# Query weights in three equal blocks, and squares added on VectorE ahead of one sum on TensorE

## What is computed

```python
def _rms(x, g):
    y = xf * lax.rsqrt(jnp.mean(xf * xf, axis=-1, keepdims=True) + EPS)
    return y * g
...
q_a = (_rms(acq, lp["mla_q_norm_g"]) @ lp["mla_w_q_up"])      # 384 -> 8 heads * (64 + 32)
ckv = _rms(ackv, lp["mla_kv_norm_g"])                          # 256
kv = (ckv_all @ lp["mla_w_kv_up"])                             # 256 -> 8 heads * (64 + 64)
o_a = _attend(...)
y = g_m * (o_m @ w_br_mlstm) + g_a * (o_a @ w_br_mla) + g_d * (o_d @ w_br_diff)
```

## Time and profile before

| | |
|---|---|
| time, median of 3 runs | 2584.89 us (2582.8 to 2585.36) |
| the profiled execution: time, span | 2583.49 us, 2581.7 us |
| PE busy | 2498.3 us, 97% of the span |
| POOL, DVE, ACT busy | 52%, 43%, 32% |
| mean granted clock of TensorE | 0.989 of full speed |
| chain that ended last | PE 89%, DVE 3%, issue 3%, ACT, POOL and DMA 1% each |

### The profile page before, as it was taken

One profiled execution on the slowest core, in us unless ns is written; L12 is line 12 of the kernel. 1 busy time (PEld: TensorE's weight loads), 2 busy tenths in 40 slices (PEclk: granted clock), 3 DMA queues, 4 the chain that ended last, 5 costly groups with the idle time before them and its releaser, 6 DMA issues.

```text
span 2581.7 us, 41451 instructions
## 1 busy us (share of the span) xinstructions
PE 2498.3 (97%) x17160; PEld 2338.0 (91%) x17160; DVE 1122.0 (43%) x1599; ACT 821.7 (32%) x1505; POOL 1348.3 (52%) x635
## 2 busy tenths in 40 slices
PE   5999999999999999999989999999999999999997
PEld 3989976888999999999978899769899999999997
DVE  5443266434455423132564525653344463222235
ACT  3251345434432303021222513554454132112031
POOL 2635530454566666666655356105445666666664
PEclk9999999999999999999999999999999999999999
DMA  6202234631122222222211022342111222222221
GB/s 267 73 17 75 68 109 145 204 123 42 45 71 74 74 74 74 74 76 76 79 57 58 29 79 68 123 164 86 62 42 58 74 74 74 74 74 75 80 75 58
DMA packets 62620, 214.64 MB, mean 83 GB/s; under 512 B 6816, under 2 KB 11360, under 8 KB 62176
## 3 DMA queue, kind: packets, MB, share of 16 engines
q1 hardware_dynamic: 56160, 202.92, 23.3%
q10 hardware_dynamic: 6272, 9.06, 1.0%
HBM read 207.14 MB, written 4.49 MB: 82 GB/s over the span
## 4 chain that ended last, share of the span: by engine, by line
PE 89%; DVE 3%; issue 3%; ACT 1%; POOL 1%; DMA 1%; SPq 1%; POOLq 1%; DVEq 0%; ACTq 0%
PE big L552 22%; PE big L555 21%; PE big L556 21%; PE four L738 6%; PE big L813 2%; PE four L634 2%; PE big L761 2%; PE four L844 2%; PE four L825 1%; PE four L783 1%; PE big L578 1%; PE big L581 1%; PE big L582 1%; DMA first_mod<-in_first 1%; PE four L773 1%
## 5 line engine op out<-in xcount | busy, mean ns | idle before, releaser
L513 POOL TENSOR_TENSOR w_hi<-raw,cst 128x1024 fp32r<-128x1024 f32 x286 | 548.6, 1918 | 1073.0 <-PE big L552 859.7
L516 POOL TENSOR_TENSOR w_lo<-raw,w_hi 128x1024 fp32r<-128x1024 f32 x286 | 737.0, 2577 | 40.8
L552 PE MATMUL big<-act_hi,w_hi 128*128 128x320 f32 x2304 | 719.0, 312 | 2.2 <-DVE act_lo L2133 1.2
L555 PE MATMUL big<-act_lo,w_hi 128*128 128x320 f32 x2304 | 714.1, 310 | 0.0
L556 PE MATMUL big<-act_hi,w_lo 128*128 128x320 f32 x2304 | 713.8, 310 | 0.0
L552 PEld LDWEIGHTS big<-act_hi,w_hi 128*128 128x128 f32 x2304 | 434.6, 189 | 10.9 <-issue 8.2
L555 PEld LDWEIGHTS big<-act_lo,w_hi 128*128 128x128 f32 x2304 | 434.7, 189 | 0.7
L556 PEld LDWEIGHTS big<-act_hi,w_lo 128*128 128x128 f32 x2304 | 434.6, 189 | 0.0
L552 PE MATMUL big<-u_hi,w_hi 128*128 128x320 f32 (+1 forms) x1024 | 319.0, 312 | 1.9 <-DVE u_lo L2152 1.9
L555 PE MATMUL big<-u_lo,w_hi 128*128 128x320 f32 (+1 forms) x1024 | 317.4, 310 | 0.0
L556 PE MATMUL big<-u_hi,w_lo 128*128 128x320 f32 (+1 forms) x1024 | 317.1, 310 | 0.0
(11 more groups left out here) (322 smaller groups left out, 4083.7 us busy)
## 6 DMA issues: line engine op xcount, KB each, us to landing
raw<-in_w SPq DMA_DIRECT2D x366, 512.0 KB, 3.5
first_mod<-in_first SPq DMA_DIRECT2D x16, 512.0 KB, 15.8
x<-in_x ACTq DMA_DIRECT2D x1, 2560.0 KB, 12.6
out_y<-x SPq DMA_DIRECT2D x8, 320.0 KB, 2.6
cst<-in_const ACTq DMA_DIRECT2D x1, 1665.0 KB, 9.0
small<-in_small ACTq DMA_DIRECT2D x2, 437.0 KB, 9.0
out_C<-c_new ACTq DMA_DIRECT2D x2, 258.0 KB
v_d<-in_past ACTq DMA_DIRECT2D x2, 256.0 KB, 3.2
```

The source lines that it names most:

```text
L513: nc.gpsimd.tensor_tensor(w_hi[:, to, :], raw[:, slot, :], ones[:, 0:1].to_broadcast([P, BLK]), ALU.mult)
L516: nc.gpsimd.tensor_tensor(w_lo[:, to, :], raw[:, slot, :], w_hi[:, to, :].bitcast(f32), ALU.subtract).then_inc(split_ready, 1)
L552: first = mm(ps, wh, ah, start=k == 0, stop=False)
L555: mm(ps, wh, al, start=False, stop=False)
```

## The change

The 18 tiles of the query weights are packed six to a block, so each of the three blocks holds two output tiles; 128x1024 blocks are still loaded, with zeros in the last quarter, and POOL splits 128x768 of them. The squares of the keys and the queries are added on DVE into `t1` (`add_squares`, behind branch tiles 2 and 4), and PE multiplies the ones by the one sum, waiting for the new semaphore `small_gathered`.

```diff
+QUP_TILES = 6
...
+                    n = P * QUP_TILES if 0 <= block - FIRST_BLOCK["qup"] < 3 else BLK
+                    nc.gpsimd.tensor_tensor(w_hi[:, to, 0:n], raw[:, slot, 0:n],
+                                            ones[:, 0:1].to_broadcast([P, n]), ALU.mult)
                     pool.drain()
-                    nc.gpsimd.tensor_tensor(w_lo[:, to, :], raw[:, slot, :], w_hi[:, to, :].bitcast(f32),
+                    nc.gpsimd.tensor_tensor(w_lo[:, to, 0:n], raw[:, slot, 0:n], w_hi[:, to, 0:n].bitcast(f32),
                                             ALU.subtract).then_inc(split_ready, 1)
...
-                    b, q = divmod(p, 8)
+                    b, q = divmod(p, per)
...
-            def small_sums(l, t, first_sq, n):
-
-                for k in range(n):
-                    pe.wait_ge(sq_ready, l * SQUARES + first_sq + k + 1)
-                    for h in range(2):
-                        last = mm(t[:, h, 0:HALF], ones, sq[:, k % 2, h * HALF:(h + 1) * HALF],
-                                  start=k == 0, stop=k == n - 1)
-                    last.then_inc(small_sum if k == n - 1 else sq_used, 1)
+            def small_sums(l, t, norm):
+
+                pe.wait_ge(small_gathered, l * 2 + norm - NORMS["kn"] + 1)
+                for h in range(2):
+                    last = mm(t[:, h, 0:HALF], ones, t1[:, h * HALF:(h + 1) * HALF], start=True, stop=True)
+                last.then_inc(small_sum, 1)
...
+                def add_squares(name, n):
+
+                    dve.wait_ge(sq_ready, l * SQUARES + FIRST_SQ[name] + 2)
+                    v.tensor_tensor(t1[:, :], sq[:, 0, :], sq[:, 1, :], ALU.add).then_inc(sq_used, 1)
+                    dve.drain()
+                    for k in range(2, n):
+                        dve.wait_ge(sq_ready, l * SQUARES + FIRST_SQ[name] + k + 1)
+                        v.tensor_tensor(t1[:, :], t1[:, :], sq[:, k % 2, :], ALU.add).then_inc(sq_used, 1)
+                        dve.drain()
+                    dve.drain().then_inc(small_gathered, 1)
+
                 def norm_behind(m):
 
+                    if m == 2:
+                        add_squares("kn", KKV)
+                    if m == 4:
+                        add_squares("qn", KQ)
```

More of the change, by code:

```diff
@@ L363, in trunk @@
         out_copied = sem("out_copied")
-        gather_done, small_sum = sem("gather_done"), sem("small_sum")
+        gather_done, small_sum, small_gathered = sem("gather_done"), sem("small_sum"), sem("small_gathered")
         row_copied, row_turned = sem("row_copied"), sem("row_turned")
@@ L512, in _ @@
                         pool.wait_ge(block_used, l * DENSE + block)
-                    nc.gpsimd.tensor_tensor(w_hi[:, to, :], raw[:, slot, :],
-                                            ones[:, 0:1].to_broadcast([P, BLK]), ALU.mult)
+                    n = P * QUP_TILES if 0 <= block - FIRST_BLOCK["qup"] < 3 else BLK
+                    nc.gpsimd.tensor_tensor(w_hi[:, to, 0:n], raw[:, slot, 0:n],
+                                            ones[:, 0:1].to_broadcast([P, n]), ALU.mult)
                     pool.drain()
-                    nc.gpsimd.tensor_tensor(w_lo[:, to, :], raw[:, slot, :], w_hi[:, to, :].bitcast(f32),
+                    nc.gpsimd.tensor_tensor(w_lo[:, to, 0:n], raw[:, slot, 0:n], w_hi[:, to, 0:n].bitcast(f32),
                                             ALU.subtract).then_inc(split_ready, 1)
@@ L529, in block_start, with project @@
                 pe.wait_ge(split_ready, l * DENSE + b + 1)
-            def project(l, uses, first_block, tiles, nk, hi, lo, n=HALF, arrived=None, more=0, tile=None):
+            def project(l, uses, first_block, tiles, nk, hi, lo, n=HALF, arrived=None, more=0, tile=None, per=8):
                 for p in range(tiles * nk):
                     m, k = divmod(p, nk)
-                    b, q = divmod(p, 8)
+                    b, q = divmod(p, per)
                     slot, col = slot_of(l, first_block + b), P * q
@@ L1014, in behind_pair_m @@
                     if p == 1:
-                        small_sums(l, two, FIRST_SQ["kn"], KKV)
+                        small_sums(l, two, NORMS["kn"])
                     if p == 2:
-                        small_sums(l, last_two, FIRST_SQ["qn"], KQ)
+                        small_sums(l, last_two, NORMS["qn"])
                 merge(l, "merge_m", om_hi, om_lo, "om", beside_gates_m, behind_pair_m)
                 project(l, USE["qup"], FIRST_BLOCK["qup"], 6, KQ, qn_hi, qn_lo,
-                        arrived=lambda k: l * SPLITS + FIRST_SPLIT["q"] + k + 1)
+                        arrived=lambda k: l * SPLITS + FIRST_SPLIT["q"] + k + 1, per=QUP_TILES)
                 project(l, USE["kvn"], FIRST_BLOCK["kvn"], 4, KKV, ckv_hi, ckv_lo, n=TK // 2,
@@ L2220, in _wide, with _pairs @@
     return w.reshape(kk // 256, 2, P, n // 512, 512).transpose(3, 0, 2, 1, 4).reshape(-1, P, BLK)
-def _pairs(tiles):
+def _pairs(tiles, per=8):
     m, _, k, _ = tiles.shape
-    s = tiles.transpose(0, 2, 1, 3).reshape(m * k // 8, 8, P, P)
-    return s.transpose(0, 2, 1, 3).reshape(-1, P, BLK)
+    s = tiles.transpose(0, 2, 1, 3).reshape(m * k // per, per, P, P)
+    s = s.transpose(0, 2, 1, 3).reshape(-1, P, per * P)
+    return np.pad(s, ((0, 0), (0, 0), (0, BLK - per * P)))
 def _blocks(i, l):
@@ L2239, in _blocks @@
     halves = [qu[:, :, a:a + ROPE // 2].reshape(Q_RANK, P) for a in (NOPE, NOPE + ROPE // 2)]
-    qall = np.concatenate(halves + [qu[:, :, :NOPE].reshape(Q_RANK, -1), np.zeros((Q_RANK, 2 * P), w.dtype)], axis=1)
+    qall = np.concatenate(halves + [qu[:, :, :NOPE].reshape(Q_RANK, -1)], axis=1)
     ku = i["mla_w_kv_up"][l].reshape(KV_RANK, H_A, NOPE + V_A)
@@ L2251, in _blocks @@
     out += [_pairs(_tiles(ckv)), merge_m[2:]]
-    out += [_pairs(_tiles(a)) for a in (qall, kn)] + [_wide(kv)]
+    out += [_pairs(_tiles(qall), QUP_TILES), _pairs(_tiles(kn)), _wide(kv)]
     out += [_pairs(_tiles(dq)), _pairs(_tiles(dk)), _wide(dv), merge(1, i["w_br_mla"][l])]
```

## The result

The changed kernel takes 2568.07 us (median of 4 runs, 2567.64 to 2568.44) against 2585.1 us for the kernel before in the same session (4 runs, 2582.8 to 2585.36): a ratio of 0.9938, interval 0.9927 to 0.995. The profiled execution has a span of 2566.3 us, 15.4 us shorter than before, at a mean clock of 0.990 (before 0.989). PE's share is still 97%: what went is idle time, records of the two sums, and time at half clock.

A forecast was written before the change was run, and what follows sets the result against it. PE, busy 97% of the span, was taken as the bound; 4.97 + 0.95 + 1.50 = 7.42 us a layer, 14.84 in two, gave 2568.65 to 2570.05 us, predicted 2569.5, range 2566.5 to 2576.5.

The forecast's parts named there:

- The wait before "kvn": PE's wait for POOL's split after the third query block: 3.91 us would become 0.39 per layer.
- the term of 0.39: PE's remaining wait before "kvn": split finished 5.67 us from the third block's start, less the block's 5.28 us.
- the estimate from the Trainium skill: At the split of "kvn": each POOL instruction waits out one 0.824 us DVE operation; PE waits 1.32 us, total 1.9 longer.
- The half clock: First nine "kvn" products run at 1.2 GHz behind the wait; full clock there would win 1.45 us per layer.
- The rival that the short waits halve the clock as well: Half clock behind the waits at "kvn" and the queries' sum costs 5.8 us in two layers: 2575.3 us; chance 0.10.
- The argument against it from the old queries' sum: The old queries' sum was said to hold a wait too, yet its window's clock stayed 1.00.
- The keys' sum: PE's sum of the keys' squares: four records for eight, no wait, gain 0.95 us of 1.91 per layer.
- The queries' sum: PE's sum of the queries' squares: 3.00 us becomes 0.95 plus a new 0.55 us wait, gain 1.50 per layer.
- The smaller splits: POOL's splits of the query blocks: 4.4 us at most within 5.28 us per block, costing PE nothing.
- its other case: If smaller splits saved no time, each of the two middle query blocks would be 0.39 us late.
- Attention: Rival: the gain is given back at the attention, 3.5 us per layer if rotary keys end 10 us later: 2576.5; chance 0.03.
- The cover: Slack between the end of DVE's rotary keys and PE's earlier arrival at the attention: 6.5 us.

The follow-up runs named there:

- blocks alone: Changed kernel with PE summing the squares as before, without `add_squares`, so only the blocks of six remain: 2576.24 us, ratio 0.997 to the kernel before.
- sevens: Changed kernel with seven query tiles to a block, so the third block has four tiles, 24 products: 2573.33 us, ratio 0.9963 to the kernel before.
- full split: Changed kernel with POOL splitting all 1024 columns of the three query blocks, zeros included: 2569.45 us, ratio 0.9945 to the kernel before.
- late additions: Changed kernel with the first addition of the queries' squares done five times: 2581.34 us, ratio 0.999 to the kernel before.
- The third square's experiment: Changed kernel with ACT writing the queries' third square into `rs`: 2570.27 us, ratio 0.9944 to the kernel before; repeated, 2568.87 us, 0.9942.
- sums alone: Changed kernel with query weights again eight tiles to a block, all 1024 columns split, additions kept: 2582.28 us, ratio 0.9992 to the kernel before.

## Why the prediction was right

**The wait before "kvn"** went as predicted: 0.21 us, not 0.39, within the bounds of 0 and 0.93. The third block's length is its cause (blocks alone, sevens). In the timeline of POOL the split of "kvn":

```profile
332.08 2.16 POOL L515 TENSOR_TENSOR w_hi<-raw,cst 128x1024 fp32r<-128x1024 f32 x1 [1.56 <-PE big L554]
334.39 2.68 POOL L518 TENSOR_TENSOR w_lo<-raw,w_hi 128x1024 fp32r<-128x1024 f32 x1
```

takes 334.39 + 2.68 - 332.08 = 4.99 us, where the working had kept the old 5.16. That is the term of 0.39 mis-sized by 0.17. The working's own sum (the split, 0.51 us around it, less the third block) gives the wait in the other traces too: full split 2.68 + 335.23 - 332.70 = 5.21, so 5.21 + 0.51 - 5.28 = 0.44 us, measured 0.44. In layer 0 of the sevens and of the late additions, timelines of POOL:

```profile
333.92 2.35 POOL L515 TENSOR_TENSOR w_hi<-raw,cst 128x1024 fp32r<-128x1024 f32 x1 [1.77 <-PE big L554]
336.40 2.61 POOL L518 TENSOR_TENSOR w_lo<-raw,w_hi 128x1024 fp32r<-128x1024 f32 x1
```

```profile
338.56 1.91 POOL L515 TENSOR_TENSOR w_hi<-raw,cst 128x1024 fp32r<-128x1024 f32 x1 [1.00 <-PE big L554]
340.60 2.68 POOL L518 TENSOR_TENSOR w_lo<-raw,w_hi 128x1024 fp32r<-128x1024 f32 x1
```

5.09 + 0.51 - 3.52 = 2.08 us, measured 2.09; and 4.72 + 0.51 is less than 5.28, and "kvn" came with no wait (15.84 us in the table, 108 x 0.147).

By the estimate from the Trainium skill (SBUF — State Buffer, "Who interferes with whom") PE would have waited 1.32 us. POOL's two instructions were longer than the 1.89 and 2.41 alone, but by 0.27 each. DVE's timeline beside them shows who waited for whom:

```profile
331.81 0.68 DVE L2069 TENSOR_TENSOR sq<-stage,cst 128x512 f32<-128x512 f32 x1
332.41 2.38 DVE L2070 TENSOR_TENSOR rs<-stage,cst 128x512 f32<-128x512 f32 x1
334.72 2.90 DVE L2071 TENSOR_TENSOR sq<-stage,cst 128x512 f32<-128x512 f32 x1
```

Each time POOL began within the last 0.4 us of an operation of DVE (331.81 + 0.68 is 0.41 behind 332.08), and it lost 0.27. DVE's next operation, 0.68 us long when undisturbed, then took 2.38 and 2.90 and ended 0.55 us behind POOL's instruction. That the two shut each other out, as that section of the Trainium skill says, agrees with this trace. What failed in the estimate is that POOL would wait out whole operations: here DVE paid, and the attention didn't wait for it (below).

**The half clock** is won: 1.41 and 1.64 us, 1.45 predicted. (Nine products at full clock, 1.55 in the working, would be 1.49 as nine of its 26 in 4.30; they took 1.66.) The rival that the short waits halve the clock as well had a chance of 0.10, and the windows show 1.00 behind both of them. The argument against it from the old queries' sum was empty, since that sum held no wait (below). The swing from short idles of which the Trainium skill tells (TensorE: Matmul & The Clock Gate, "A second HAM failure mode: psum-queue depth-cycling") isn't seen behind 0.21 and 0.38 us here, but these are single idles, and frequent ones were not run.

**The keys' sum** won 1.07 us, 0.95 predicted: the working misread what a record costs. It divided 1.91 us by eight, but the product behind the sum starts only 0.03 us after the sum's last record, so 1.91 us holds seven distances. By the durations, 2.31 us for eight records and 1.24 for four, records stand (2.31 - 1.24)/4 = 0.27 us apart before and after, and four fewer are 1.07 us. The addition is ready long before: it starts at 273.95 and takes 0.82, and PE comes at 276.19. In the timeline of DVE, with the third square from that of ACT behind it:

```profile
273.95 0.82 DVE L2020 TENSOR_TENSOR t<-sq 128x640 f32<-128x640 f32 x1 [0.18 <-issue]
...
295.15 0.82 DVE L1645 SCALAR_TENSOR_TENSOR y<-stage,big 128x640 f32<-128x640 f32 x1 [9.47 <-PE big L558]
296.16 0.83 DVE L2020 TENSOR_TENSOR t<-sq 128x640 f32<-128x640 f32 x1 [0.19 <-issue]
297.79 0.82 DVE L2024 TENSOR_TENSOR t<-t,sq 128x640 f32<-128x640 f32 x1 [0.81 <-ACT sq L1094]
```

```profile
297.02 0.74 ACT L1094 ACTIVATE sq<-acq 128x640 f32<-128x640 f32 x1 [3.28 <-DVE t L2020]
```

**The queries' sum** won 3.00 - 1.32 = 1.68 us, 1.50 predicted. The same misreading stands here: eleven distances of 0.27 us and 0.03 are 3.00, so the old sum was all work, and its wait of 0.13 us for the third square wasn't there. Eight fewer records are 2.15 us, of which the new wait takes 0.38 and the first record behind it 0.10 more than the others (four records last 1.34 there, 1.24 in the keys' sum). The chain is the predicted one. Its first addition ended 296.99 - 295.97 = 1.02 us behind the branch tile (1.11 assumed), and the two hops to ACT and back took 0.03 us each (0.07 assumed). So the wait was 0.38, not 0.55. The 1.11 let the addition wait for the end of POOL's split. No such hold is seen: the addition starts at 296.16, and the split ends at 293.84 + 2.41 = 296.25 (timeline of POOL), so that part of the size owes something to luck.

```profile
293.84 2.41 POOL L518 TENSOR_TENSOR w_lo<-raw,w_hi 128x1024 fp32r<-128x1024 f32 x1
```

The third square's experiment, which takes ACT out of the chain, removes that wait; the late additions show what it would cost if longer.

**The smaller splits** "cost PE nothing" holds. That they were worth something the working gave only as its other case, the two middle blocks 0.39 us late each; measured, it is 0.5 us a layer in all.

**Attention.** The cover was 6.5 us in the working. DVE's rotary keys end at 345.97 and the attention starts at 353.75, so 7.8 us are left; nothing was given back there.

```profile
344.81 1.16 DVE L2082 TENSOR_SCALAR k_a<-key_rope,cst 64x768 f32<-64x768 f32 x2
```

In sum: 15.96 us won at the three places, 14.84 predicted, less about 0.5 for clock in a stage that the change doesn't touch; 2568.07 us, 2569.5 predicted. A stage that varies by 2 us makes the closeness of the total in part luck; the mechanism is borne out at the three places.

## What to carry to other kernels

Where a consumer's block is short, the producer that is released by its start has no time to work: cut the blocks so that each lasts at least as long as the preparation of the next, and look at the clock behind the wait, which can be a second gain (here it fell behind waits of 1.92 and 3.25 to 3.82 us, and held behind 1.68). Adding on an idle engine ahead of a matrix sum pays if the addition is ready before TensorE comes; if it isn't, each hop in that chain is TensorE's own time. What one record costs is read from two groups of different length, not from a group's time divided by its records. Compare kernels by stages, from start to start of the same product, since a total can hide one microsecond of gain behind two of clock.

## What was not expected of the hardware

The same stage, with the same instructions, took 26.5 to 28.9 us at mean clocks of 0.87 to 0.76, and profiles of programs that differ elsewhere by 0.5 us a layer came out 2 us apart through it. Behind waits of much the same length the low clock lasted differently: behind 3.74 us, "kvn" to attention took 19.24 us with the sums alone, and 18.04 behind 3.75 us before; behind 1.92 us it took 18.21, behind 1.68 us 16.66. Beside POOL, operations of DVE of 0.68 us took 2.38 and 2.90 us, and POOL's own instructions only 0.27 us more.
